# Two transformer blocks on one core: sums of squares on GpSimd and VectorE, transposes in place of diagonal products, c spread on the chip, clearings spread, and pairs of four-column products ahead of long runs

## The reference

```
# block 1, layer l:  c_act = silu(c);  mod = c_act @ w_ada[l] + b_ada[l]   (9 x 1024)
x = x + 0.5 * gate(0) * swiglu(norm_mod(x, 0))          # d_ff 2816
x = x + gate(1) * mixer(norm_mod(x, 1))                 # LRU, stick-breaking and forgetting attention
x = x + 0.5 * gate(2) * swiglu(norm_mod(x, 2))
# block 2, layer l:  mod = silu(c2) @ w_mod[l] + b_mod[l]   (6 x 1024)
x = x + gt1 * (group_rmsnorm(four mixers(h)) @ w_out[l])  # pooling, chunk, top-64 and latent attention
x = x + gt2 * swiglu(...)
norm_mod(h, j) = rms(h) * g * (1 + scale_j) + shift_j;   rms(h) = h * rsqrt(mean(h * h) + 1e-6)
```

## Time and profile before

| what | us |
|---|---|
| three timed runs | 1592.84, 1593.21, 1593.38 (median 1593.21) |
| the profiled execution's own time | 1594.71 |
| its span, first to last instruction | 1592.9 |
| TensorE busy in the span | 1558.1 (98%), 13290 matmul records |
| VectorE / ScalarE / GpSimd busy | 1285.8 / 905.1 / 240.4 |
| mean granted TensorE clock | 0.998 |
| moved by DMA | 403 MB, 253 GB/s in the mean |

### The profile page before, as it was taken

How to read it: one execution, slowest core, us unless ns; L and a number is a source line. 1 busy time by engine, 2 the same in 40 slices (tenths; PEclk the granted TensorE clock), 3 DMA queues, 4 the chain that set the end, 5 groups by cost and what they waited for, 6 DMA issues and landing times.

```text
span 1592.9 us, 32431 instructions
## 1 busy us (share of the span) xinstructions
PE 1558.1 (98%) x13290; PEld 1533.4 (96%) x13290; DVE 1285.8 (81%) x1933; ACT 905.1 (57%) x1563; POOL 240.4 (15%) x254
## 2 busy tenths in 40 slices
PE   4999999999999999999999999999999999999998
PEld 3999999999999999999999999999999999999998
DVE  6788898888888878888887898788888888786553
ACT  5455457665554655459665445667555466664553
POOL 4122000022210222000112231001221010021100
PEclk9999999999999999999999999999999999999999
DMA  9999974459888889864569998434899873457761
GB/s 342 345 335 336 324 273 156 162 189 347 311 315 283 291 304 326 295 231 153 185 226 332 314 318 270 163 132 147 305 333 335 312 243 130 141 190 238 237 215 41
DMA packets 110996, 403.11 MB, mean 253 GB/s; under 512 B 12562, under 2 KB 12818, under 8 KB 110720
## 3 DMA queue, kind: packets, MB, share of 16 engines
q1 hardware_dynamic: 109280, 395.87, 70.9%
q0 software_dynamic: 1568, 5.17, 1.2%
HBM read 399.94 MB, written 1.05 MB: 252 GB/s over the span
## 4 chain that ended last, share of the span: by engine, by line
PE 87%; DVE 8%; ACT 2%; issue 1%; DMA 1%; SPq 0%; DVEq 0%; ACTq 0%
PE PS L558 86%; DVE SCR L1695 2%; DVE WL L1692 2%; DVE SCR L1692 1%; DMA SCR<-in_x 1%; ACT WH L1216 1%; DVE SCR L2049 1%; DVE ring L1718 1%; DVE SMALL L2048 1%; ACT SCR L1503 0%; PE PS L1159 0%; PE PS L1055 0%; DVE MOD L1689 0%; DVE SCR L1689 0%; DVE SMALL L2088 0%
## 5 line engine op out<-in xcount | busy, mean ns | idle before, releaser
L1692 DVE TENSOR_TENSOR WL<-ring,WH 128x1024 fp32r<-128x1024 f32 (+1 forms) x508 | 604.2, 1223 | 184.7 <-ACT WH L1216 184.4
L558 PE MATMUL PS<-HH,WH 128*128 128x256 f32 (+1 forms) x2640 | 628.7, 280 | 2.2 <-ACT WH L1216 2.2
L558 PE MATMUL PS<-HL,WH 128*128 128x256 f32 (+1 forms) x2640 | 614.8, 277 | 0.0
L1216 ACT ACTIVATE WH<-ring 128x1024 fp32r<-128x1024 f32 (+1 forms) x508 | 511.4, 1049 | 46.8 <-PE PS L558 44.1
L558 PEld LDWEIGHTS PS<-HH,WH 128*128 128x128 f32 x2640 | 496.7, 188 | 3.3 <-ACT WH L1216 2.3
L558 PEld LDWEIGHTS PS<-HL,WH 128*128 128x128 f32 x2640 | 491.7, 188 | 0.6
L558 PE MATMUL PS<-HH,WL 128*128 128x256 f32 (+1 forms) x2640 | 375.8, 278 | 1.0 <-DVE WL L1692 0.7
L1718 DVE CUSTOM_DVE_ANT_0 ring<-ring,CB,VC 128x1024 f32<-128x1024 f32 x238 | 331.1, 1408 | 11.2 <-DMA ring<-in_ada 11.2
L558 PEld LDWEIGHTS PS<-HH,WL 128*128 128x128 f32 x2640 | 337.0, 189 | 1.8 <-DVE WL L1692 1.8
L558 PE MATMUL PS<-AH,WL 128*128 128x256 f32 x1056 | 292.4, 277 | 0.5 <-DVE WL L1692 0.5
L558 PE MATMUL PS<-AH,WH 128*128 128x256 f32 x1056 | 292.6, 277 | 0.0
(11 more groups left out here) (214 smaller groups left out, 1457.4 us busy)
## 6 DMA issues: line engine op xcount, KB each, us to landing
ring<-in_up SPq DMA_DIRECT2D x176, 512.0 KB, 5.7
ring<-in_ada SPq DMA_DIRECT2D x144, 512.0 KB, 6.1
ring<-in_ffn SPq DMA_DIRECT2D x132, 512.0 KB, 4.9
ring<-in_mod SPq DMA_DIRECT2D x96, 512.0 KB, 5.8
ring<-in_down SPq DMA_DIRECT2D x88, 512.0 KB, 5.7
ring<-in_win SPq DMA_DIRECT2D x64, 512.0 KB, 5.7
ring<-in_wout SPq DMA_DIRECT2D x32, 512.0 KB, 4.2
ring<-in_winv SPq DMA_DIRECT2D x8, 512.0 KB, 4.2
```

What stands on the lines that cost most here:

```text
L558: return e.matmul(out, lhsT, rhs, start=start, stop=stop, skip_group_check=skip)
L1216: e.activation(half_of(i)[0], slot_of(("half", i, 0))[:, 0:w], ACT.Copy).then_inc(s_hi, 1)
L1692: return e.tensor_tensor(out, a, b, op)
```

## The change

What it does:

- Norms: square_sums() adds all eight chunks on GpSimd; ScalarE rounds the sum to SH, VectorE takes the rest SL (square_rest()), and sum_squares() multiplies the float32r ones with SH and SL. It stands in the second early() panel instead of the first. ScalarE takes hi_half(2 * UNIT0[m] + 3) ahead of R, and the last chunk's square ahead of its gain.
- Tiles: unit_rows() scales the tile itself on VectorE, turned_out() is then a transpose. In mixer1 both of the last two stand at c = 5.
- c: the first spread load of CB is dropped; TensorE transposes 128 copies of each column of silu(c), and ScalarE copies the result to CB. Ahead of the first FFN TensorE makes eight float32 products of 256 columns whose result nothing reads.
- Clearings: one behind each remainder, f = 4 to 11 of n = 5.
- Pairs: narrow() makes two products with four weight columns. They stand ahead of unit 2 of every sublayer but the first, ahead of f = 1, 2 and 4 of the first FFN, and in round 0 of each output projection ahead of c = 6 (mixer1) or c = 7 (mixer2).
- mixer1: forget() gives its first 16 products in two groups behind the gates; ScalarE does stick_weights(1) ahead of hi(u0 + 11).

```diff
-            spread_c(0)
             def square_sums(m):
-                for c in range(1, KD - 1):
+                for c in range(1, KD):
...
+            cleared = [(buf, 0.0) for buf in (QH, KH, SAK, PU, *TSA)] + [(buf, -BIG) for buf in TCA]
...
                     e.tensor_tensor(AL[:, f, :], G6[:, 3 + f % 3, :], AH[:, f, :].bitcast(F32), ALU.subtract).then_inc(s_al, 1)
+                    if n == 5 and 4 <= f < 12:
+                        buf, fill = cleared[f - 4]
+                        e.memset(buf, fill).then_inc(s_zero2, 1)
...
+            def narrow(out, moving):
+                for _ in range(2):
+                    mm(out[0:4, :], WFH[:, 0, 0:4], moving)
...
                 e.wait_ge(s_hi, i + 1)
+                if paced:
+                    e.wait_ge(s_hh, 8 * n + 1)
+                    narrow(out, HH[:, 0, 0:S])
...
             def sum_squares(m):
-                e.wait_ge(s_psum, 6 * m)
+                e.wait_ge(s_sql, m)
                 if m > 1:
                     e.wait_ge(s_r, m - 1)
-                mm(PS[:, 6, 0:256], ones, SQ[:, KD - 2, :], start=True, stop=False)
-                e.wait_ge(s_sq, 8 * m)
-                mm(PS[:, 6, 0:256], ones, SQ[:, KD - 1, :], start=False, stop=True).then_inc(s_ss, 1)
+                mm(PS[:, 6, 0:256], onesr[:, :], SH[:, :], start=True, stop=False)
+                mm(PS[:, 6, 0:256], onesr[:, :], SL[:, :], start=False, stop=True).then_inc(s_ss, 1)
...
+                if p == 1:
+                    sum_squares(n)
                 e.wait_ge(s_lo, i + 1)
...
                 if p == 0:
-                    sum_squares(n)
                     k = KD - 1
...
-                cols(2 * UNIT0[n] + 2 * u, n, PS[:, b, 0:256], u == 2)
+                cols(2 * UNIT0[n] + 2 * u, n, PS[:, b, 0:256], u == 2, u == 2)
...
-                    last = mm(PS[:, turn_bank(n, o), 256 + 128 * c:384 + 128 * c], OT[o % 4][:, 128 * c:128 * c + 128], DG[o % 2])
+                    last = e.transpose(PS[:, turn_bank(n, o), 256 + 128 * c:384 + 128 * c], OT[o % 4][:, 128 * c:128 * c + 128], ident1)
...
+                    if r == 0 and c == (6 if SUBS[n][0] == "mix1" else 7):
+                        narrow(out, YH[:, ks[0], :])
...
-                                 f == (2 if n > 0 else 0) and part == 0)
+                                 f == (2 if n > 0 else 0) and part == 0, part == 0 and f in ((2,) if n > 0 else (1, 2, 4)))
...
-                columns(n, 3, 1, 0, lambda: (gate(0), gate(1)))
-                columns(n, 4, 0, 3, lambda: (gate(2), gate(3)))
-                forget()
+                columns(n, 3, 1, 0, lambda: (gate(0), gate(1), forget(range(4))))
+                columns(n, 4, 0, 3, lambda: (gate(2), gate(3), forget(range(4, KD))))
+                forget_rest()
...
-                    4: (lambda: turned_out(n, o0 + 2),),
-                    5: (lambda: turned_out(n, o0 + 3),),
+                    5: (lambda: turned_out(n, o0 + 2), lambda: turned_out(n, o0 + 3)),
...
+            e.wait_ge(s_cc, 1)
+            for k in range(KD):
+                last = e.transpose(PS[:, k // 4, 128 * (k % 4):128 * (k % 4) + 128], vec("c", k).to_broadcast([128, 128]), ident)
+            last.then_inc(s_cspread, 1)
...
+            for c in range(8):
+                mm(PS[:, 6, 0:256], ident, X[:, c % KD, :])
...
             def norm(m):
+                e.wait_ge(s_psum, 7 * m)
+                e.activation(SH[:, :], SQ[:, KD - 1, :], ACT.Copy).then_inc(s_sqh, 1)
+                hi_half(2 * UNIT0[m] + 3)
                 e.wait_ge(s_ss, m)
...
-                hi_half(2 * UNIT0[m] + 3)
...
+                if c == KD - 1 and n + 1 < NSUB:
+                    e.wait_ge(s_x, 8 * n + c + 1)
+                    square(n + 1, c)
+                    gained(n + 1, c)
+                    return
...
+                stick_weights(1)
                 hi(u0 + 11)
-                stick_weights(1)
...
-            e.activation(CB[:, :], CB[:, :], ACT.Silu).then_inc(s_cb, 1)
             lnexp()
+            e.wait_ge(s_cspread, 1)
+            e.activation(CB[:, :], PS[:, 0:2, :].rearrange("p a s -> p (a s)"), ACT.Copy).then_inc(s_cb, 1)
...
+            def square_rest(m):
+                e.wait_ge(s_sqh, m)
+                tt(SL[:, :], SQ[:, KD - 1, :], SH[:, :].bitcast(F32), ALU.subtract).then_inc(s_sql, 1)
...
-            def diagonal(n, o):
+            def unit_rows(n, o):
                 e.wait_ge(s_oss, o + 1)
-                if o >= OUT0[n] + 2:
-                    e.wait_ge(s_ot, o - 1)
-                ts(DG[o % 2], ident1, SM_[:, 114 + o % 2:115 + o % 2], None, ALU.mult, None).then_inc(s_od, 1)
+                ts(OT[o % 4], OT[o % 4], SM_[:, 114 + o % 2:115 + o % 2], None, ALU.mult, None).then_inc(s_od, 1)
```

More of the change, by code:

```diff
@@ L181, in vec @@
             return VC[:, VEC[name] + i:VEC[name] + i + n]
-        ident, ones, bd, ntri, partner, rev, causal, nones = (const(n) for n in (
-            "ident", "ones", "bd", "ntri", "partner", "rev", "causal", "nones"))
+        ident, bd, ntri, partner, rev, causal, nones = (const(n) for n in (
+            "ident", "bd", "ntri", "partner", "rev", "causal", "nones"))
         eps = const("eps")
-        ident1 = identr[:, :].bitcast(F32)
+        ident1, ones1 = identr[:, :].bitcast(F32), onesr[:, :].bitcast(F32)
         one = const("one")
@@ L279, in build @@
         JK = scr(256)
-        DG = [scr(128) for _ in range(2)]
         Scratch.at = 0
@@ L780, in gate, with forget, forget_rest @@
                     last.then_inc(s_gate, 1)
-                def forget():
-                    wfh, wfl = v3(WFH[:, l, :], KD), v3(WFL[:, l, :], KD)
-                    e.wait_ge(s_wfh, 2)
-                    for k in range(KD):
+                def forget(ks):
+                    wfh = v3(WFH[:, l, :], KD)
+                    for k in ks:
                         mm(PS[0:4, 6, 0:256], wfh[:, k, :], HH[:, k, 0:S], start=k == 0, stop=False)
                         mm(PS[0:4, 6, 0:256], wfh[:, k, :], HL[:, k, 0:S], start=False, stop=False)
+                def forget_rest():
+                    wfl = v3(WFL[:, l, :], KD)
+                    e.wait_ge(s_wfh, 2)
                     for k in range(KD):
@@ L873, in recurrence_sums @@
                     for k in range(4):
-                        last = mm(PS[:, 7, 0:256], ones, GT[:, k, :], start=k == 0, stop=k == 3)
+                        last = mm(PS[:, 7, 0:256], ones1, GT[:, k, :], start=k == 0, stop=k == 3)
                     last.then_inc(s_gnss, 1)
@@ L987, in latent_sums @@
                             mm(PS[:, 6, 256 + t:257 + t], MSQ[:, k, 128 * t:128 * t + 128], one, start=k == 0, stop=k == 1)
-                    mm(PS[:, 6, 0:256], ones, MSQ[:, 2, :]).then_inc(s_mss, 1)
+                    mm(PS[:, 6, 0:256], ones1, MSQ[:, 2, :]).then_inc(s_mss, 1)
                 def keys():
@@ L1295, in ffn @@
                         e.wait_ge(s_const_rest, 16)
-                        for exact, k in ((identr, "ident"), (causalr, "causal"), (sbposr, "sbpos")):
+                        for exact, k in ((identr, "ident"), (causalr, "causal"), (sbposr, "sbpos"), (onesr, "ones")):
                             e.activation(exact[:, :], const(k), ACT.Copy).then_inc(s_exact, 1)
@@ L1995, in mixer1 @@
                 share(n, 2)
-                diagonal(n, o0)
-                diagonal(n, o0 + 1)
+                unit_rows(n, o0)
+                unit_rows(n, o0 + 1)
                 lo(u0 + 11)
@@ L2008, in mixer1 @@
                 partial(n, 3)
-                diagonal(n, o0 + 2)
-                diagonal(n, o0 + 3)
+                unit_rows(n, o0 + 2)
+                unit_rows(n, o0 + 3)
                 lo_half(2 * u0 + 24)
@@ L2184, in mixer2 @@
                 tile_rest(n, o0 + 2)
-                diagonal(n, o0 + 4)
+                unit_rows(n, o0 + 4)
                 gates(n)
@@ L2195, in mixer2 @@
                 partial(n, 1)
-                diagonal(n, o0 + 5)
+                unit_rows(n, o0 + 5)
                 maxima2(a0 + 5, 1)
@@ L2201, in mixer2 @@
                 tile_rest(n, o0 + 4)
-                diagonal(n, o0 + 6)
+                unit_rows(n, o0 + 6)
                 partial(n, 3)
@@ L2208, in mixer2 @@
                 tile_rest(n, o0 + 5)
-                diagonal(n, o0 + 7)
+                unit_rows(n, o0 + 7)
                 partial(n, 5)
```

33 lines of the change are left out of this document (17 added, 16 removed).

## The result

The changed kernel takes 1602.93 us (median of 14 runs, 1592.80 to 1618.02), the kernel before 1594.24 in the same rounds (14 runs): a ratio of 1.0041, 95% interval 1.0023 to 1.0060. It is slower by about half a per cent where I forecast 1579.1 with a chance of 0.93 for faster. Medians and ranges in this document take in every execution, while the ratios leave out those over 1.5% above the fastest of their kernel (one here, three of the twelve of c3 and two of the ten of q1), which ran at the same granted clock as the rest, so that in these three the ratio shows less loss than the medians (here 1602.93/1594.24 = 1.0055). The profiled execution took 1605.55, its span is 1603.7. The times of the changed kernel are not spread evenly: most stand near 1592.8, 1598.6, 1605.5, 1612.1 and 1618.0, in steps of 5.8 to 6.9 us.

The account below looks back on a forecast made before the run. TensorE, 87% of the chain, was taken to bound the kernel. Terms 5.6 + 4.0 + 0.85 + 1.7 + 2.5 − 3.6 + 1.1 + 1.9 = 14.1 us gave a forecast of 1579.1 (ratio 0.991), range 1574 to 1586.

Parts of the forecast that it names:

- Pairs set the slow pace: Rival, FFN runs: with float32 sums gone the phase may fall slow, 37 us more, 1616; chance 0.04.
- elsewhere the runs are fast already: Pairs term: outside the 119 slow products in each mixer 1, pairs find nothing else to win.
- Norm sums: Nine norms: two float32r products replace two float32 ones, 0.63 each, 5.6 us gained; longer chain covered.
- the longer chain is late: Rival, norms: the sum waits 0.5 to 1 us in each, giving 1583.6 to 1588; chance 0.12.
- Turned tiles: Mixers, 24 tiles: 2 records replace 4, 0.22 each; 4.0 us gained after losses at waits.
- two of eight stand ahead of the waits: Turned tiles in mixer 2: two precede waits for VectorE and ScalarE, which don't shorten; 0.9 us lost over both.
- stick_weights(1) and forget(): Mixer 1: earlier exponentials remove a TensorE wait, 0.85 us; split products cover WL waits and turn fast, 1.7 us.
- VectorE keeps the mixers: Rival, mixers: VectorE sets them all, so gains of tiles, exponentials and forget() (6.6) go: 1585.7; chance 0.11.
- Clearings: FFN n = 5: spreading them removes MOD's 4.29 us, the wait (0.62) and its slow pace (1.9); 2.5 us gained.
- Pairs: First FFN, unit 2, output rounds: 16 pairs cost 3.6 us and win 1.1 in mixer 1's slow products.
- Start: Before the first FFN: x 1.5 us earlier, added products cost 3.5, no low clock; 1.9 us gained.
- half clock in the added products: Rival, start: added products take 7 us instead of 3.5, giving 1582.6; chance 0.11.

Follow-up runs that it names:

- c3: Changed kernel without pairs, plus one float32r product with four moving columns ahead of the float32r sums in each norm: median 1599.80 us, ratio 1.0000.
- q1: Changed kernel without pairs, with a four-column float32 product ahead of the sums, that product and sums moved behind one more 258-column product: 1604.62 us, 1.0020.
- b1: Kernel before with nothing but the change of the norm sums: median 1588.68 us, ratio 0.9965.
- m1: Kernel before with nothing but the turned tiles: median 1596.49 us, ratio 0.9999.
- a3: Changed kernel with float32 sums of squares as before and no pairs, all else of the change kept: median 1589.39 us, ratio 0.9966.
- a4: Kernel before with nothing but the 16 pairs: median 1596.89 us, ratio 1.0004.
- m2: a3 with VectorE's tile scaling and HL work behind the mixers cut, part of the computation left out: 1585.38 us, ratio 0.9948.
- a1: Changed kernel without any pair of four-column products, all else kept: median 1588.52 us, ratio 0.9963.
- a2: Changed kernel with the norms as before (float32 sums of squares), pairs and all else kept: median 1591.04 us, ratio 0.9974.
- s1: Changed kernel without pairs, with a four-column float32 product ahead of each norm's sums, minus the eight added start products: 1586.53 us, ratio 0.9949.
- r1: a3 with one more 258-column product, result unread, ahead of the last product of the fourth early panel: median 1611.01 us, ratio 1.0096.
- r2: a3 with two more 258-column products ahead of the last product of the fourth early panel: median 1590.12 us, ratio 0.9979.
- r3: a2, which has the pairs, with two more 258-column products ahead of the last product of the fourth early panel: 1626.63 us, ratio 1.0192.
- p1: a1 with one four-column float32 product inside the fourth early panel, at another distance from unit 2 in each sublayer: one run, 1604.23 us.
- c1: a3 with the float32 sums moved ahead of one more 258-column product, nothing added: median 1594.26 us, ratio 1.0002.

## Why the prediction was wrong

- **The step that failed** is in the rival "Pairs set the slow pace", to which I gave 0.04 with the words "what sets the phase is not shown", and in the term for pairs, "elsewhere the runs are fast already". I took the pace of 113.3 ns behind the norms as given. It rested on the place at which unit 2 begins, which the float32 sums kept at 7 or 3. The rival had the effect (float32 sums gone, phase falls the other way) and its size per product (4.4 ns, measured 4.45) right. What it missed is that two parts act together: N lets the place wander, P makes places 1, 4, 5 and the even stretch slow. A chance of 0.04 was too small for something whose cause I had called not shown. Slow products: 4,100 more, 18.3 us; the forecast had 3.2 gained there. That is 21.5 of the 24.9 by which the span missed 1578.8.
- **Norm sums**, 5.6: b1 shows a span 7.4 shorter, of which 442 fewer slow products are 2.0: 5.4. Right, and the longer chain is covered as argued; "the longer chain is late" did not happen.
- **Turned tiles**, 4.0 (24 × 0.22 is 5.3, not 5.4, so 3.9): 1.5 (0 in each first mixer, 0.75 to 0.8 in each second). The step "two of eight stand ahead of the waits" was too kind: in the first mixers nothing arrives (in m1 the wait behind two of the four tiles grows by the 0.45 that they save, and a new wait stands on the way out), and in the second about half of the 8 × 0.22 = 1.8 is lost.
- **stick_weights(1) and forget()**, 0.85 and 1.7: none of it arrives. The waits of the earlier trace rows are gone, but TensorE then waits 0.61 for WH at 262.70 and 0.37 + 0.36 for HL on the way out; against the start's 2.6, n = 2 and n = 5 of a3 begin 2.46 and 2.51 earlier. "VectorE keeps the mixers", at 0.11, is what happened in the first mixers, with its price of up to 6.6 mostly paid: the four mixers of a3 gave about 1.5 with the pace taken out, all of it in the second kind.
- **Clearings**, 2.5: in a3, n = 6 begins 5.14 earlier than before and n = 5 began 2.51 earlier: 2.6. The number is right, but 1.9 of it is luck. I had said that the wait for WL started the slow pace. In a4, b1 and m1, where the clearings stand as before, TensorE has the same wait of 0.46 us for WL and VectorE the same 4.29 us on MOD, and the 429 products behind the wait go at the fast pace in all three. So the wait alone doesn't start it; against those traces the clearings save only the wait, 0.6. With the clearings spread no VectorE instruction on MOD is over 0.165 us (the changed kernel, a3 and m2).
- **Pairs**, −3.6: a4's span is 2.0 longer with 474 fewer slow products (2.1), so −4.1; between a1 and the changed kernel it is 1603.7 − 1594.3 − 1,494 × 4.45 ns = 2.8. The size was right. The gain of 1.1 in the rounds did not come: of the two rounds of mixer1 the changed kernel has that of n = 1 fast and that of n = 4 slow, a2 the reverse, a4 both fast.
- **Start**, 1.9: 2.6. The added products ran at full clock (3.4 us for 16 records); "half clock in the added products" did not happen. The Trainium skill ("TensorE: Matmul & The Clock Gate", PE-mode transpose) says that transposes don't count as activity for the clock; in s1, where only the one-column products with c stand between them and the weights, the granted clock is 0.68 again behind a 2.2 us gap, so that run can't tell whether the transposes or the gap keep the clock down.

What is shown: the place tells the pace (180 of 180), and edits of one or two products that move the place turn the pace (r1, r2 and r3). Whether the place itself is the cause, or a state of the engine that the steps of 258 columns only make visible, no run tells. What stays open: why there are two paces at all, what sets the one of n = 0, which no panels of 258 columns precede (slow in a1, p1, q1 and r2, fast in the other 16 traces), what keeps the pace for 1,500 products once it is taken, and why the float32 sums of 256 columns leave the nine sublayers at one place (a3, a4, c1) or at two, 7 and 3 (before, a2, m1, m2), while the float32 product with four moving columns lets them differ. That an execution differs from the next by 6.6 us fits a place that falls otherwise in one sublayer; only profiled executions show their places.

## What to carry to other kernels

When a stream of equal matmuls is the whole span, read its pace as a count per window before and after a change, for busy time and granted clock can be the same to the digit while 18 us go. A forecast for such a kernel needs the pace of every long run in its sum, with the chance that any edit ahead of it flips it; compare variants by their sorted times and by traces, not by one median. The fastest kernel here is the change without its pairs and with one small float32 product in each norm (c2_tiny_float32, 0.9941 of before, 0.9921 to 0.9961; 18 below the changed kernel).

## What the runs showed of the hardware

- One float32r product of 128x128 by 128x256, each with a new weight load, issues every 113.3 ns or every 117.8 ns at the same full clock, and holds the one or the other for up to 1,583 products (n = 0 of a3 and c2 fast, of a1 and r2 slow).
- The Trainium skill ("TensorE: Matmul & The Clock Gate", Back-to-back issue gap) gives columns over 2.4 GHz plus 2.5 ns for a product by itself, an estimate of 109 ns here, and for streams with weight loads 81 ns at 128 columns and 131 at 512. It has one pace for a shape; the traces of this study have two for 256 columns, both between 81 and 131, and neither of them 109, which the prediction took as the gap of a stream.
- Products of 258 columns step in a cycle of eight, mean 120.8 ns in the kernel before, one of them 125; the step at which they stop tells the pace of what follows.
